# A one-core transformer kernel on Trainium2: position bias in one matmul pass of 64 columns, its scratch reordered, latent transposes one step earlier, mask additions behind them

## The chip, the core and the metric

The kernel runs on one core of one Trainium2 chip. The metric is device time in microseconds (us), the median of several runs. The engines of the core are TensorE (PE, with its weight loads as PEld), VectorE (DVE), ScalarE (ACT), GpSimd (POOL) and SyncE (SP); each works through its own instructions in order and waits on semaphores for the others.

## The reference, cut to what matters

The program is two transformer blocks on 256 rows of width 2048: projections, attention heads of several kinds, a feed-forward part, and a final output. Everything is float32. The part that the change touches is in the second block, the sparse attention "a" (`dsa_attention`), whose logits get a bias that depends on the distance between query and key through 32 buckets and a table of 32 buckets by 8 heads:

```
bias = rel_table[t5_bucket(pq[:, :, None] - pk)]
logits = jnp.where(valid, logits + bias, -jnp.inf)
```

and `valid` keeps the 64 keys with the highest index score (and only earlier keys). Beside it runs the latent attention "b", whose query and key/value latents are normed and multiplied:

```
qb = rms_norm(bcq, g) @ w_b_uq
kv = rms_norm(bckv, g) @ w_b_ukv
```

## The kernel before

**Products.** Each weight matrix is streamed in groups of 2 x 128 rows by 512 columns (512 KB). SP loads a group into one of four RAW slots. ACT copies it rounded into WH (`split`, L958), DVE subtracts to get the rest WL (`split`, L1409), and PE makes three 512-column matmuls per tile of it, high by high, high by low and low by high (L604 to L606), 12 in a group. That is how a float32 product is reached from the reduced format fp32r. ACT and DVE split group p + 4 in the step in which PE works on group p, so that PE has up to four groups in hand. `prod_free` and the pairs of PSUM banks 0 to 3 carry finished products to their evacuation (L963, L972). Every other piece of work (heads, norms, transposes, bias) is hung between groups: a table or an `if p == ...` in each engine's part says behind which group `p` it stands. No scheduler decides anything: the order is the order of the code.

**Position bias.** In the stage `gates_ret` (two passes of a loop, 16 groups each) twelve bias steps run behind groups 2, 4, 7, 10, 12 and 15 (`BIAS_AT`). For each, POOL writes the distances DI of 8 queries by 128 keys for four partition groups (L509), DVE turns them into one-hot rows OH with two instructions (L1586, L1587) two groups earlier, PE multiplies OH by the table REL (L748), ACT copies the result from PSUM to BE (L1132) and issues its store to `bias_scratch` in DRAM (L1134). REL holds the table rounded (part 0) and its remainder (part 1), 32 columns each. For each half of OH both parts are multiplied into the same 32 PSUM partitions: four matmuls a step. Before its copy ACT waits for the landing of the previous store (`bias_stored`).

**Reading it back.** When the heads "c" are finished, at the start of stage `b_proj` (24 groups), ACT issues four loads of the whole bias into BIAS, 128 queries by 8 heads by 384 (L1279).

**Stage `gates_b0`** (8 groups, p = 0 to 7) follows `b_proj`. DVE ends the search for the 64 best keys in steps 0 and 1, makes the mask in step 2 (L1804, L1805) and adds it to both halves of BIAS in steps 3 and 4 (L1813), after `bias_loaded`. The six tiles of the latents are transposed by PE behind groups 4, 5 and 6 (L645), copied by ACT (L999) and finished by DVE (L1438) into LATT in the same steps. Behind the stage PE waits until all six are done (`tr_lo`), before `merge_c`. ACT applies Silu to the b gate, 2048 elements a partition, in step 2 (L1330), and in step 7 evacuates the product with Sigmoid (L972).

**Stage `merge_c`** is a loop of two passes of 24 groups, four "a" heads each. For the first head POOL needs both mask additions (`sel_ready` 2) and writes QK (L560, L562); PE transposes QK behind group 0 (L665), ACT copies it to QKT (L1010), PE computes the scores behind group 1 (L685), DVE adds BIAS and finds the maximum (L1454 to L1461), ACT takes Exp (L1018). The four head steps of PE hang at groups 0, 1, 3, 4.

ACT can evaluate only functions of the table set that is loaded: where the next one is of another set, the compiler places an ACT_TABLE_LOAD. Silu, Sigmoid and Exp are in different sets here.

## Time and profile before

| what | us |
|---|---|
| median of 3 runs | 2494.52 (2493.90 to 2494.82) |
| profiled execution | 2494.93 |
| its span, first to last instruction | 2493.1 |
| PE busy | 2472.4 (99%) |
| DVE busy | 1502.3 (60%) |
| ACT busy | 1232.2 (49%) |
| POOL busy | 235.9 (9%) |

The share of busy time is that of the whole span. A matmul's busy time contains its latency: a 512-column matmul shows 0.39 us, but the next one begins 0.23 us after it, so that the distance between starts, not the duration, is what one costs. The rows of the trace come in the section before the prediction. A row of the timeline gives start, duration, engine, line, operation, what is written and read, shapes and how many; in brackets stands the idle time before it on its engine and what ended it.

### The profile page before, as it was taken

The page shows a single profiled execution, that of the slowest core. Times are in us where ns is not written, and L with a number is a line of the kernel's source. Part 1 is how long each engine was busy: PE and PEld are TensorE (multiplying, and loading weights), DVE is VectorE, ACT ScalarE, POOL GpSimd, SP SyncE. Part 2 cuts the span into 40 slices and gives each one's busy share as a digit, 9 for nine tenths or more (in the row PEclk, how much of TensorE's full clock was granted, in tenths as well). Part 3 has the DMA queues.
Part 4 walks back from the last instruction along what each step waited for, and adds up shares of the span by engine and source line. Part 5 has one row for each costly group of instructions (what it writes and reads, how often), then busy time and mean ns, then how long its engine had stood idle before and what let it go on. Part 6 is the DMA issues. An engine that isn't in the chain of part 4 may idle for free.

```text
span 2493.1 us, 35940 instructions
## 1 busy us (share of the span) xinstructions
PE 2472.4 (99%) x11882; PEld 2052.0 (82%) x11882; DVE 1502.3 (60%) x1800; ACT 1232.2 (49%) x1632; POOL 235.9 (9%) x277
## 2 busy tenths in 40 slices
PE   7999999999999999999999999999999999999999
PEld 6888888878888888888888888888887788877887
DVE  4444545486656777777777776444457655554564
ACT  4444555545445444444444445454547555555443
POOL 0012124231000000000000000010101000432000
PEclk9999999999999999999999999999999999999999
DMA  6555555566655555555555556554564545544655
GB/s 230 194 185 171 174 171 175 170 217 204 211 186 177 186 188 189 186 186 191 187 186 191 186 187 210 204 185 169 175 206 163 175 161 180 165 155 148 226 183 164
DMA packets 130194, 461.08 MB, mean 185 GB/s; under 512 B 14288, under 2 KB 17616, under 8 KB 129232
## 3 DMA queue, kind: packets, MB, share of 16 engines
q1 hardware_dynamic: 121536, 443.60, 53.1%
q10 hardware_dynamic: 8592, 16.58, 2.0%
q8 instruction: 44, 0.72, 0.1%
q14 instruction: 22, 0.18, 0.0%
HBM read 454.36 MB, written 5.77 MB: 185 GB/s over the span
## 4 chain that ended last, share of the span: by engine, by line
PE 97%; DVE 1%; ACT 1%; DMA 0%; issue 0%; ACTq 0%; POOL 0%; SPq 0%; POOLq 0%; DVEq 0%
PE PS L604 21%; PE PS L606 21%; PE PS L605 21%; PE PS L809 13%; PE PS L811 7%; PE PS L833 3%; PE PS L835 3%; PE PS L834 3%; PE PS L685 1%; PE PS L702 1%; PE PS L665 1%; PE PS L645 1%; DVE WL L1409 0%; PE PS L748 0%; PE PS L693 0%; ACT WH L958 0%
## 5 line engine op out<-in xcount | busy, mean ns | idle before, releaser
L1409 DVE TENSOR_TENSOR WL<-RAW,WH 128x1024 fp32r<-128x1024 f32 x842 | 1055.9, 1257 | 933.9 <-ACT WH L958 929.4
L958 ACT ACTIVATE WH<-RAW 128x1024 fp32r<-128x1024 f32 x842 | 890.2, 1059 | 1146.6 <-PE PS L606 755.0
L604 PE MATMUL PS<-WH,HT 128*128 128x512 f32 (+1 forms) x1820 | 726.8, 399 | 3.2 <-DVE LATT L1438 1.3
L606 PE MATMUL PS<-WH,HT 128*128 128x512 f32 (+1 forms) x1820 | 710.0, 390 | 0.0
L605 PE MATMUL PS<-WL,HT 128*128 128x512 f32 (+1 forms) x1820 | 708.6, 389 | 0.0
L809 PE MATMUL PS<-HT,WH 128*128 128x512 f32 x1408 | 498.2, 399 | 0.0
L604 PEld LDWEIGHTS PS<-WH,HT 128*128 128x128 f32 x1820 | 342.4, 188 | 77.1 <-issue 8.9
L606 PEld LDWEIGHTS PS<-WH,HT 128*128 128x128 f32 x1820 | 342.1, 188 | 72.4
L605 PEld LDWEIGHTS PS<-WL,HT 128*128 128x128 f32 x1820 | 342.9, 188 | 66.0
L811 PE MATMUL PS<-HT,WL 128*128 128x256 f32 x1408 | 395.4, 281 | 0.0
L809 PEld LDWEIGHTS PS<-HT,WH 128*128 128x128 f32 x1408 | 264.6, 188 | 65.7
L811 PEld LDWEIGHTS PS<-HT,WL 128*128 128x128 f32 x1408 | 266.0, 189 | 0.3
L833 PE MATMUL PS<-WH,ACTT 128*128 128x512 f32 x352 | 137.2, 390 | 0.0
L835 PE MATMUL PS<-WH,ACTT 128*128 128x512 f32 x352 | 137.1, 389 | 0.0
L834 PE MATMUL PS<-WL,ACTT 128*128 128x512 f32 x352 | 137.0, 389 | 0.0
L604 PE MATMUL PS<-WH,U 128*128 128x512 f32 x320 | 129.7, 405 | 0.0
L606 PE MATMUL PS<-WH,U 128*128 128x512 f32 x320 | 125.2, 391 | 0.0
L605 PE MATMUL PS<-WL,U 128*128 128x512 f32 x320 | 124.7, 390 | 0.0
L440 POOL TENSOR_TENSOR MS<-MS,CONST 128x2 f32<-128x2 f32 (+1 forms) x8 | 1.6, 200 | 1068.7 <-ACT PS L990 784.6
L835 PEld LDWEIGHTS PS<-WH,ACTT 128*128 128x128 f32 x352 | 66.1, 188 | 14.1
L833 PEld LDWEIGHTS PS<-WH,ACTT 128*128 128x128 f32 x352 | 66.1, 188 | 13.9
L834 PEld LDWEIGHTS PS<-WL,ACTT 128*128 128x128 f32 x352 | 66.1, 188 | 13.4
(242 smaller groups left out, 1922.2 us busy)
## 6 DMA issues: line engine op xcount, KB each, us to landing
RAW<-w_stream SPq DMA_DIRECT2D x842, 512.0 KB, 3.3
X<-x_in SPq DMA_DIRECT2D x2, 1024.0 KB, 6.6
MEMR<-mem_in ACTq DMA_DIRECT2D x1, 2048.0 KB, 11.3
X<-x_in ACTq DMA_DIRECT2D x4, 512.0 KB, 4.3
x_scratch<-X ACTq DMA_DIRECT2D x4, 512.0 KB, 4.1
X<-x_scratch ACTq DMA_DIRECT2D x1, 2048.0 KB, 8.1
out<-X ACTq DMA_DIRECT2D x8, 256.0 KB, 3.1
bias_scratch<-BE ACTq DMA_DIRECT2D x12, 128.0 KB, 2.4
```

What stands on the lines that cost most here:

```text
L604: pe.matmul(o, hi, WH[:, slot, kk, 0:cols], start=k == 0, stop=False)
L605: pe.matmul(o, hi, WL[:, slot, kk, 0:cols], start=False, stop=False)
L606: ins = pe.matmul(o, lo, WH[:, slot, kk, 0:cols], start=False, stop=k == nq * GK - 1)
L645: ins = pe.transpose(PS[:, 4 + at % 4, t * P:(t + 1) * P], src[:, t, k * P:(k + 1) * P], ident)
L665: ins = pe.transpose(PS[0:n, 4 + a, c * S + t * P:c * S + (t + 1) * P], QK[:, a, t, c * P:c * P + n], ident)
L809: pe.matmul(PS[:, half + f, :], WH[:, slot, kk, f * P:(f + 1) * P], HT[:, k, :, :], start=k == 0, stop=False, skip_group_check=True)
L811: ins = pe.matmul(PS[:, half + f, 0:S], WL[:, slot, kk, f * P:(f + 1) * P], HT[:, k, 0, :], start=False, stop=k == KT - 1, skip_group_chec ...
L833: pe.matmul(o, hi, WH[:, slot, kk, :], start=k == 0, stop=False)
L834: pe.matmul(o, hi, WL[:, slot, kk, :], start=False, stop=False)
L835: ins = pe.matmul(o, lo, WH[:, slot, kk, :], start=False, stop=k == FT - 1)
L958: act.activation(WH[:, g.slot(j)], RAW[:, g.slot(j)], ACT.Copy).then_inc(hi_split, 1)
L1409: dve.tensor_tensor(WL[:, s], RAW[:, s], WH[:, s].bitcast(F32), ALU.subtract).then_inc(lo_split, 1)
```

## The change

It does five things.

1. A bias step multiplies OH once by both parts of REL as 64 columns, two matmuls instead of four. The two partial results lie in 64 PSUM partitions and are not added there. ACT copies 64 partitions of the same length, and the store is 256 KB instead of 128 KB.
2. `bias_scratch` is ordered by query, row, segment, key. The store writes pieces of 128 elements (512 B). The load reads 3072 elements in one row (12 KB) per partition, for part 0 into BIAS and for part 1 into the new tile BIASL: eight loads of 384 KB instead of four. BIASL lies where JUNK lay, so the squares of the latents write to LSQ.
3. DVE adds BIASL to BIAS in two instructions, in steps 10 and 12 of `b_proj`.
4. The latent transposes stand behind groups 3, 4 and 5 of `gates_b0` (on PE, ACT and DVE). The mask additions stand in steps 5 and 6, the first behind the last LATT.
5. ACT's Silu of the b gate stands in step 7 of `gates_b0`, behind the Sigmoid evacuation, instead of in step 2.

```diff
@@ -223,6 +223,8 @@
         BIAS = sb("BIAS", [P, REL_HEADS, CAUS], F32, at_u2)
+        BIASL = sb("BIASL", [P, REL_HEADS, CAUS], F32, at_u1)
+        LSQ = sb("LSQ", [P, 832], F32, at_u1 + 12 * KB)
         LATT = sb("LATT", [P, 6, 2, S], F32R, at_sgx + 4 * KB)
 
         SG = {"merge_moba": sb("SG_MOBA", [P, T, CH], F32, at_u2), "merge_c": sb("SG_C", [P, T, CH], F32, at_u2 + 12 * KB),
@@ -243,7 +245,7 @@
 
         DI = sb("DI", [P, 8, P], I32, at_x)
         OH = sb("OH", [P, 2, 8, P], F32R, at_x + 4 * KB)
-        BE = sb("BE", [32, 8, P], F32, at_x + 12 * KB)
+        BE = sb("BE", [64, 8, P], F32, at_x + 12 * KB)
@@ -263,7 +265,7 @@
-        bias_scratch = nc.dram_tensor("bias_scratch", (32, 3, 32, P), F32, kind="Internal").ap()
+        bias_scratch = nc.dram_tensor("bias_scratch", (32, 64, 3, P), F32, kind="Internal").ap()
         x_scratch = nc.dram_tensor("x_scratch", (S, D), F32, kind="Internal").ap()
 
         def con(name, rows=P):
@@ -744,9 +746,8 @@
                 pe.wait_ge(onehot, k.count(1))
                 pe.wait_ge(bias_copied, k.count(1))
                 for b in range(2):
-                    for part in range(2):
-                        ins = pe.matmul(PS[0:32, 4 + b, :], REL[:, part, :],
-                                        OH[:, k.base % 2, 4 * b:4 * b + 4, :].rearrange("p q s -> p (q s)"), start=part == 0, stop=part == 1)
+                    ins = pe.matmul(PS[0:64, 4 + b, :], REL[:].rearrange("p a n -> p (a n)"),
+                                    OH[:, k.base % 2, 4 * b:4 * b + 4, :].rearrange("p q s -> p (q s)"), start=True, stop=True)
                 ins.then_inc(bias_done, 1)
             pe.wait_ge(rel_lo, 1)
             product_loop("gates_ret", 2, [(GD, HT)] * 2, bias_step)
@@ -894,9 +895,9 @@
             products("b_proj", [(GD, HT)] * 3, 0, index_step)
 
             def latent_tiles(_, p):
-                if 4 <= p < 7:
+                if 3 <= p < 6:
                     pe.wait_ge(lat_rows, 1)
-                    transposes("lat", PB, [2 * p - 8, 2 * p - 7])
+                    transposes("lat", PB, [2 * p - 6, 2 * p - 5])
 
             def a_step(i, p):
                 r = p // 6
@@ -1129,9 +1130,10 @@
                 k = At(s, i, len(BIAS_AT))
                 act.wait_ge(bias_done, k.count(3))
                 act.wait_ge(bias_stored, k.count(1) * 16)
-                act.activation(BE[:].rearrange("p (b q) s -> p b (q s)", b=2), PS[0:32, 4:6, :], ACT.Copy).then_inc(bias_copied, 1)
+                act.activation(BE[:].rearrange("p (b q) s -> p b (q s)", b=2), PS[0:64, 4:6, :], ACT.Copy).then_inc(bias_copied, 1)
                 act.wait_ge(bias_copied, k.count(2))
-                act.dma_start(bias_scratch[:, s % 3, ds(i * 16 + s // 3 * 8, 8), :], BE[:]).then_inc(bias_stored, 16)
+                act.dma_start(bias_scratch[ds(i * 16 + s // 3 * 8, 8), :, s % 3, :].rearrange("q r k -> r q k"),
+                              BE[:]).then_inc(bias_stored, 16)
 
             act.wait_ge(head_out, RET0 + 4 + 1)
             act.dma_start(MEMR[:], rows(mem_in)).then_inc(mem_loaded, 16)
@@ -1275,9 +1277,11 @@
 
             act.wait_ge(head_out, C0 + 4 + 1)
             act.wait_ge(bias_stored, 16 * (NBIAS + 1))
-            for g in range(4):
-                act.dma_start(BIAS[32 * g:32 * g + 32, :, :].rearrange("p h (s k) -> p h s k", s=3),
-                              bias_scratch[8 * g:8 * g + 8].rearrange("h s p k -> p h s k")).then_inc(bias_loaded, 16)
+            for part, dst in enumerate((BIAS, BIASL)):
+                for g in range(4):
+                    r = 32 * part + 8 * g
+                    act.dma_start(dst[32 * g:32 * g + 32].rearrange("p h n -> p (h n)"),
+                                  bias_scratch[:, r:r + 8].rearrange("p h s k -> p (h s k)")).then_inc(bias_loaded, 16)
 
             squares = [(PAC[:, h // 4, t, h % 4 * P:(h % 4 + 1) * P], MST[:, 0, t, h:h + 1]) for h in range(8) for t in range(T)]
             squares += [(PAC[:, 2, t, h * P:(h + 1) * P], MST[:, 1, t, h:h + 1]) for h in range(2) for t in range(T)]
@@ -1300,9 +1304,9 @@
                     for src, acc in squares[4 * (p - TOPK_AT - 1):4 * (p - TOPK_AT)]:
                         link(act.activation(JK[:, 0:P], src, ACT.Square, scale=P ** -0.5, accum_out=acc))
             def latent_squares(t):
-                act.activation(JUNK[:, t, 0:512], PB[:, t, 0:512], ACT.Square, scale=512 ** -0.5, accum_out=MS[:, t:t + 1])
-                act.activation(JUNK[:, t, 512:768], PAC[:, 7, t, KV_LAT], ACT.Square, scale=1 / 16.0, accum_out=MS[:, 2 + t:3 + t])
-                return act.activation(JUNK[:, t, 768:832], PAC[:, 7, t, KPE], ACT.Square, scale=192 ** -0.5,
+                act.activation(LSQ[:, 0:512], PB[:, t, 0:512], ACT.Square, scale=512 ** -0.5, accum_out=MS[:, t:t + 1])
+                act.activation(LSQ[:, 512:768], PAC[:, 7, t, KV_LAT], ACT.Square, scale=1 / 16.0, accum_out=MS[:, 2 + t:3 + t])
+                return act.activation(LSQ[:, 768:832], PAC[:, 7, t, KPE], ACT.Square, scale=192 ** -0.5,
                                       accum_out=MS[:, 4 + t:5 + t])
             act.wait_ge(prod_free, 2 + PROD0["b_proj"])
             for p in range(3 * GD):
@@ -1326,10 +1330,10 @@
                         steps(p)
 
             def latent_steps(p):
-                if p == 2:
+                if p == 7:
                     act.activation(PB[:, :, PB_Z:PB_Z + W], PB[:, :, PB_Z:PB_Z + W], ACT.Silu).then_inc(gate_ready, 1)
-                elif 4 <= p < 7:
-                    transposed("lat", LATT, [2 * p - 8, 2 * p - 7], "lat")
+                elif 3 <= p < 6:
+                    transposed("lat", LATT, [2 * p - 6, 2 * p - 5], "lat")
             gates_b("gates_b0", 0, 1, latent_steps)
 
             def a_step(i, p):
@@ -1787,6 +1791,10 @@
                                                            op0=ALU.mult, op1=ALU.add)
                         link(ins)
                     dve.sem_inc(idx_sum, 1)
+                if p in (10, 12):
+                    dve.wait_ge(bias_loaded, 128)
+                    half = slice((p - 10) * 2, (p - 10) * 2 + 4)
+                    link(dve.tensor_tensor(BIAS[:, half], BIAS[:, half], BIASL[:, half], ALU.add))
                 if p == TOPK_AT - 2:
                     dve.wait_ge(lat_rstd, 1)
                     for t in range(T):
@@ -1805,11 +1813,10 @@
                     link(dve.scalar_tensor_tensor(out=SC[:, 0:CAUS], in0=left[:, 0:CAUS], scalar=-NEG, in1=con("mask"),
                                                   op0=ALU.mult, op1=ALU.add))
 
-                if 4 <= p < 7:
-                    transposed("lat", LATT, [2 * p - 8, 2 * p - 7], "lat")
-                if p in (3, 4):
-                    dve.wait_ge(bias_loaded, 64)
-                    half = BIAS[:, (p - 3) * 4:(p - 2) * 4]
+                if 3 <= p < 6:
+                    transposed("lat", LATT, [2 * p - 6, 2 * p - 5], "lat")
+                if p in (5, 6):
+                    half = BIAS[:, (p - 5) * 4:(p - 4) * 4]
                     dve.tensor_tensor(half, half, SC[:, 0:CAUS].unsqueeze(1).broadcast_to([P, REL_HEADS // 2, CAUS]),
                                       ALU.add).then_inc(sel_ready, 1)
             dve.wait_ge(sel_ready, 2)
```

What stands in a row on the engines, before and after. On PE, one bias step between two groups (`gates_ret`). Before:

```order
L744 ISA
L748 MATMUL PS<-OH,REL 32x512 x4
L591 REGISTER_ALU
L604 MATMUL PS<-WH,HT 128x512
L605 MATMUL PS<-WL,HT 128x512
L606 MATMUL PS<-WH,HT 128x512
```

After:

```order
L746 ISA
L749 MATMUL PS<-OH,REL 64x512 x2
L593 REGISTER_ALU
L606 MATMUL PS<-WH,HT 128x512
L607 MATMUL PS<-WL,HT 128x512
L608 MATMUL PS<-WH,HT 128x512
```

Four matmuls have become two, and nothing else moved there. On DVE, `gates_b0` from the mask on (LATT is the latents' tile, SC the mask). Before:

```order
L1804 TENSOR_SCALAR OF<-OF 128x384
L1805 SCALAR_TENSOR_TENSOR SC<-OF,CONST 128x384
L1409 TENSOR_TENSOR WL<-RAW,WH 128x1024
L1813 TENSOR_TENSOR BIAS<-BIAS,SC 128x1536
L1409 TENSOR_TENSOR WL<-RAW,WH 128x1024
L1438 SCALAR_TENSOR_TENSOR LATT<-PS,PARAM,LATT 128x256 x2
L1813 TENSOR_TENSOR BIAS<-BIAS,SC 128x1536
L1409 TENSOR_TENSOR WL<-RAW,WH 128x1024
L1438 SCALAR_TENSOR_TENSOR LATT<-PS,PARAM,LATT 128x256 x2
L1409 TENSOR_TENSOR WL<-RAW,WH 128x1024
L1438 SCALAR_TENSOR_TENSOR LATT<-PS,PARAM,LATT 128x256 x2
L1409 TENSOR_TENSOR WL<-RAW,WH 128x1024
```

After:

```order
L1812 TENSOR_SCALAR OF<-OF 128x384
L1813 SCALAR_TENSOR_TENSOR SC<-OF,CONST 128x384
L1413 TENSOR_TENSOR WL<-RAW,WH 128x1024
L1442 SCALAR_TENSOR_TENSOR LATT<-PS,PARAM,LATT 128x256 x2
L1413 TENSOR_TENSOR WL<-RAW,WH 128x1024
L1442 SCALAR_TENSOR_TENSOR LATT<-PS,PARAM,LATT 128x256 x2
L1413 TENSOR_TENSOR WL<-RAW,WH 128x1024
L1442 SCALAR_TENSOR_TENSOR LATT<-PS,PARAM,LATT 128x256 x2
L1820 TENSOR_TENSOR BIAS<-BIAS,SC 128x1536
L1413 TENSOR_TENSOR WL<-RAW,WH 128x1024
L1820 TENSOR_TENSOR BIAS<-BIAS,SC 128x1536
L1413 TENSOR_TENSOR WL<-RAW,WH 128x1024
```

Each LATT pair stands one split earlier, and both mask additions stand behind the last pair, with one split left. On ACT, the end of `gates_b0` and the head of the `merge_c` loop (SGX is the Sigmoid evacuation, PB the b gate under Silu, QKT the first head's operand). Before:

```order
L972 ACT_TABLE_LOAD
L972 ACTIVATE SGX<-PS 128x1024
L1096 UNCONDITIONAL_BRANCH
L1096 ISA
L957 ISA
L958 ACTIVATE WH<-RAW 128x1024
L1004 ISA
L1010 ACTIVATE QKT<-PS,PARAM 128x256 x2
L957 REGISTER_ALU
L958 ACTIVATE WH<-RAW 128x1024
L1015 REGISTER_ALU
L1018 ACT_TABLE_LOAD
```

After:

```order
L973 ACT_TABLE_LOAD
L973 ACTIVATE SGX<-PS 128x1024
L1334 ACT_TABLE_LOAD
L1334 ACTIVATE PB<-PB 128x2x1024
L1097 UNCONDITIONAL_BRANCH
L1097 ISA
L958 ISA
L959 ACT_TABLE_LOAD
L959 ACTIVATE WH<-RAW 128x1024
L1005 ISA
L1011 ACTIVATE QKT<-PS,PARAM 128x256 x2
L958 REGISTER_ALU
```

Between the Sigmoid and the first split of the loop there now stand Silu and two table loads. The load that stood ahead of Exp in the loop's first head has moved to the loop's head, ahead of the first split, in both passes.

## Rows read from the trace of the kernel before

**Rows 1.** The chain that ended last, by engine, from the page.
```profile
PE 97%; DVE 1%; ACT 1%; DMA 0%; issue 0%; ACTq 0%; POOL 0%; SPq 0%; POOLq 0%; DVEq 0%
```

**Rows 2.** Timeline, PE and PEld: first bias step; weight loads of first and second.
```profile
504.69 1.09 PE L748 MATMUL PS<-OH,REL 128*32 128x512 f32 x4
505.62 0.40 PE L604 MATMUL PS<-WH,HT 128*128 128x512 f32 x1
...
504.51 0.75 PEld L748 LDWEIGHTS PS<-OH,REL 128*32 128x32 f32 x4
...
510.85 0.80 PEld L748 LDWEIGHTS PS<-OH,REL 128*32 128x32 f32 x4
```

**Rows 3.** Timeline, DVE and POOL between the first and the second one-hot.
```profile
503.18 1.29 DVE L1587 SCALAR_TENSOR_TENSOR OH<-DI,CONST,OH 128x1024 fp32r<-128x1024 int32 x1
504.68 4.06 DVE L1409 TENSOR_TENSOR WL<-RAW,WH 128x1024 fp32r<-128x1024 f32 x2 [0.22 <-DVE OH L1587]
...
504.78 2.88 POOL L509 TENSOR_TENSOR DI<-POSB 128x1024 int32<-128x1024 int32 x1 [5.65 <-DVEq L1590]
...
509.44 1.28 DVE L1587 SCALAR_TENSOR_TENSOR OH<-DI,CONST,OH 128x1024 fp32r<-128x1024 int32 x1
```

**Rows 4.** Timeline, the third bias step: its one-hot and its first weight load.
```profile
517.96 1.29 DVE L1587 SCALAR_TENSOR_TENSOR OH<-DI,CONST,OH 128x1024 fp32r<-128x1024 int32 x1
...
519.96 0.80 PEld L748 LDWEIGHTS PS<-OH,REL 128*32 128x32 f32 x4
```

**Rows 5.** Timeline, second pass of the loop: ACT's first split, seventh one-hot and step.
```profile
549.22 1.06 ACT L958 ACTIVATE WH<-RAW 128x1024 fp32r<-128x1024 f32 x1 [1.36 <-PE PS L606]
...
552.24 1.29 DVE L1587 SCALAR_TENSOR_TENSOR OH<-DI,CONST,OH 128x1024 fp32r<-128x1024 int32 x1
...
553.67 0.80 PEld L748 LDWEIGHTS PS<-OH,REL 128*32 128x32 f32 x4
```

**Rows 6.** Landing of the bias stores (page, median us) and of BIAS's four loads.
```profile
bias_scratch<-BE ACTq DMA_DIRECT2D x12, 128.0 KB, 2.4
...
DMA to landing us min/median/max: 4.9/9.3/16.8
```

**Rows 7.** Timeline, DVE's split of step 11 of `b_proj`.
```profile
1884.69 1.22 DVE L1409 TENSOR_TENSOR WL<-RAW,WH 128x1024 fp32r<-128x1024 f32 x1 [2.59 <-ACT WH L958]
```

**Rows 8.** Timeline, `gates_b0` into `merge_c`: PE, DVE's second mask addition, POOL's QK.
```profile
1944.65 0.49 PE L604 MATMUL PS<-WH,HT 128*128 128x512 f32 x1 [1.26 <-DVE LATT L1438]
...
1950.70 0.81 PE L685 MATMUL PS<-QKT 128*128 128x128 f32 x4
...
1938.51 1.75 DVE L1813 TENSOR_TENSOR BIAS<-BIAS,SC 128x1536 f32<-128x1536 f32 x1
...
1941.83 0.62 POOL L562 TENSOR_TENSOR QK<-PAC,MST 128x256 f32 x1
```

**Rows 9.** Timeline, ACT there; then ACT at the loop head of `a_proj`.
```profile
1943.49 1.06 ACT L958 ACTIVATE WH<-RAW 128x1024 fp32r<-128x1024 f32 x1 [1.42 <-PE PS L606]
...
1945.86 1.03 ACT L972 ACTIVATE SGX<-PS 128x1024 f32<-128x1024 f32 x1
...
1948.67 0.82 ACT L1010 ACTIVATE QKT<-PS,PARAM 128x256 f32<-128x256 f32 x2
...
1654.95 1.92 ACT L1256 ACTIVATE PB<-PB 128x2048 f32<-128x2048 f32 x1
1656.88 1.28 ACT L958 ACT_TABLE_LOAD   x1
1658.18 1.06 ACT L958 ACTIVATE WH<-RAW 128x1024 fp32r<-128x1024 f32 x1
```

**Rows 10.** Timeline, ACT's first split in the second pass of `merge_c`.
```profile
2023.14 1.06 ACT L958 ACTIVATE WH<-RAW 128x1024 fp32r<-128x1024 f32 x1 [1.89 <-PE PS L606]
```

**Rows 11.** Timeline, PE's first group of the program and what follows it.
```profile
17.36 0.80 PE L604 MATMUL PS<-WH,HT 128*128 128x512 f32 x1 [1.22 <-DVE HT L1438]
...
22.65 0.84 PE L645 MATMUL PS<-CONST,ROWS 128*128 128x128 f32 x4
```

## The prediction

> **What bounds the kernel now.** I read the page first. The chain that ended last is PE in 97% of the span [rows 1], so the end moves only with what PE issues and with what PE waits for. Busy time overstates a matmul, so I take distances between starts from PE's timeline. In the rows of the first bias step, see that PE goes from the bias matmuls to the next product without a gap, and how close the one-hot of DVE ends before PE wants it [rows 2, 3]. Then I read the one place in the touched stages where PE is idle, the end of `gates_b0` [rows 8], and what ACT does there [rows 9].
>
> **Two matmuls less in each bias step.** Four bias matmuls take PE from 504.69 to 505.62, 0.93 us, so one costs 0.23 [rows 2]. The number of columns that stream is 512 before and after; the weights become 64 columns wide, and weight loads lie beside the matmul ahead of them. So a step saves 2 x 0.233 = 0.47 us, and twelve steps 5.6 us, if PE finds its operands in time.
>
> **It will not, in three steps.** The first one-hot ends at 503.18 + 1.29 = 504.47, and PE's weight load follows at 504.51, 0.04 later. It normally stands 0.23 ahead of its matmul, here 0.18, so this step is already at its limit [rows 2, 3]. The second one-hot ends at 509.44 + 1.28 = 510.72, 6.25 after the first, and PE loads at 510.85 [rows 2, 3]. What fills these 6.25 us? After the one-hot DVE does two splits, the second of which ends at 504.68 + 4.06 = 508.74. POOL's distances end at 504.78 + 2.88 = 507.66, and 1.08 later the split ends, which is about one split. So DVE's second split stood until POOL was done [rows 3]. Nothing in this chain waits for PE, and the change takes nothing out of it. PE will now need 6.39 - 0.47 = 5.92 us between these two steps. It would load at 510.38 but gets the one-hot at 510.72 + 0.04: late by 0.38, less 0.05 that the load may be short, 0.33.
>
> The Trainium skill (SBUF — State Buffer, on the shared port pair) says that a VectorE operation with two SBUF inputs and a GpSimd operation exclude each other for the whole instruction. The trace agrees (the split ends 1.08 after POOL). A proportional sharing would let DVE move ahead with PE, and the bias steps would then give the full 5.6.
>
> In the second pass ACT begins late: its split at 549.22 [rows 5] follows PE's group that ended two groups before the bias matmul at 553.67 + 0.23 = 553.90. A group is 2.73, half of 510.85 + 0.23 - 505.62 [rows 2], so it ended at 548.44. ACT was held there by the evacuation, the copy to BE, the store and the turn of the loop, which begin with the end of group 15, before the bias step. They do not get shorter while PE arrives 0.47 sooner. The seventh one-hot ends at 552.24 + 1.29 = 553.53, PE's load now stands at 553.67 and would stand at 553.20 [rows 5]: late by 0.33 again, after the same 0.05. The eighth step follows after two groups as the second does, and pays the same 0.33. Together 1.0 us.
>
> The other steps have room: the third one-hot ends at 519.25, the load is at 519.96, 0.71 later [rows 4]. There the one-hot follows splits that follow PE's own groups, with no bias step between, so the distance stays. Steps 5 and 11 come two groups after another and lose 6.25 - 5.92 = 0.33 of that 0.71. **Bias stage: 5.6 - 1.0 = 4.6 us less.**
>
> **Copy and store.** ACT's copy has the same length in each partition, 1.0 us (as the Sigmoid of that size, [rows 9]). The store becomes 512 pieces of 512 B. It landed in 2.4 us before; a load of 768 such pieces needed at least 4.9 [rows 6]. In proportion between them I take 4 us. ACT waits for it before the next copy, at the closest 5.92 less about 1.2 for copy and issue, 4.7 later. Nothing waits then. Beyond that, ACT's splits queue behind it. The issue itself may last 0.2 longer, which would count in the seventh step alone.
>
> **Loads and additions.** Eight loads of 12 KB rows take the place of four of 512 B pieces: twice the bytes, a twelfth of the pieces. The last of the four landed after 16.8 us [rows 6], beside the weight stream and with no wait of PE. The new ones are needed at step 10 of `b_proj`, ten groups of 2.73 us after the issue. DVE's additions have the size of a mask addition, 1.75 us [rows 8], and each stands in a gap of 2.59 [rows 7]. Nothing is queued in it, so they cost nothing; without the gap they would take their 1.75 from four groups in hand. I take zero, between -0.5 (less time in the issue on ACT) and +2.
>
> **The wait for LATT goes.** PE stood 1.26 us behind `gates_b0` until the last LATT [rows 8]. With the transposes one step earlier and DVE's mask additions behind, the last LATT is done near 1940.6 (estimate: ACT's copy behind PE's group 5 at 1937.3, a split, a pair), and PE goes on at 1943.3. That alone gives 1.3.
>
> **What is late next.** POOL makes the first head's QK after the second mask addition. Before, the addition ended at 1940.26 and QK at 1941.83 + 0.62 = 1942.45, 2.2 later [rows 8]. Now two additions and a split stand behind the last LATT, so the second ends near 1945.1 and QK near 1947.3, while PE wants it behind group 0 of `merge_c`, at 1946.0. So PE gives back the 1.3 there.
>
> Then comes ACT. Its last split in `gates_b0` stays at 1943.49, since PE's work up to there is the same. Sigmoid's table is loaded, Sigmoid ends at 1945.86 + 1.03 = 1946.89 [rows 9]. The order of the changed kernel then shows: table, Silu, table, split, QKT. At the head of `a_proj` ACT did Silu, table, split in one run: 1.93 from Silu to the table load, 1.30 from the load to the split [rows 9]. So: 1946.89 + 1.30 + 1.93 + 1.30 = 1951.42 for the split, 0.97 more to QKT (1.06 less the overlap), 0.82 for it, and PE can compute scores near 1953.3. Before it did at 1950.70, with QKT ready since 1949.49 [rows 8, 9]. **Cost 2.6 us**, and it swallows the waits for LATT and QK. Nothing later regains it: PE has no other wait in `merge_c`. The second pass loads its table in a gap of 1.89 ahead of the first split, so it costs nothing [rows 10], as the load needs only ACT itself.
>
> The Trainium skill (ScalarE: Activation LUTs, What ACT_TABLE_LOAD costs) prices a switch at 2.66, with a drain of 1.38 behind the load. The rows show the next operation 1.30 after it [rows 9]. By the page two more switches (and the one before Sigmoid unchanged) would make the cost 5.4.
>
> **Sum.** 2494.93 (profiled) - 4.6 + 2.6 = 2492.9. The median of the runs is 0.4 below the profiled one: 2492.5.
>
> **The rivals.** *The moved Silu is covered* (a load runs while ACT waits or the scores have more room than I see). Then only POOL's QK holds PE and the stage costs 0, so the time is 2494.5 - 4.6 = 2489.9, or 2488.9 if the bias steps pay no waits either. Against it: ACT's run is a plain sum of measured pieces, 3.8 us beyond its end of before, with 1.2 of room. For it: 1950.12 is reached with pieces from another stage.
>
> *PE's clock falls.* After the long wait at the start the first group took 22.65 - 17.36 = 5.29 us instead of 2.73, so its spacing fits 1.2 GHz instead of 2.4 [rows 11]. A wait of 1.26 left it at the higher level [rows 8]. The new wait before the scores, 2.6 with 1.3 shortly before, lies between. If it decides beyond 1.26, one group costs 2.6 more: 2495.1, slower than before.
>
> *The stores hold ACT.* If the pieces of 512 B land like the median load (9.3, [rows 6]), ACT stands 4.6 us at each of the four close steps, and with 0.7 of room PE loses up to 3.9 each: above 2500. It begins at a landing of 5.4. Against it: the share of a queue of four loads is in that median.
>
> *It does less than it says*: the 64-column matmul costs as much as two (0.23 more in each of 24). Then 2498. Weight loads of 128 columns cost nothing beside matmuls elsewhere, so hardly.
>
> *The page's price for a switch* gives 2495.3.
>
> **How the numbers follow.** Forecast 0.68, its own range 2491.3 to 2493.7 (bias waits 0.4 to 1.6, Silu's chain 2.2 to 3.0). Silu covered 0.13. Clock 0.08. Stores 0.03. Wide matmul 0.02. The page's price 0.02. The rest, 0.04, lies on both sides. The range for 8 in 10 goes to the covered Silu at 2489.9 and the clock at 2495.1: 2489.8 to 2495.3. A measurement of this kernel can tell about 0.2% (5 us) from no change. Faster by that, below 2489.5: half of the covered case and some rest, 0.10. Slower, above 2499.5: stores and rest, 0.05. Same: 0.85.
>
> **What would show it.** In the changed trace: bias steps 0.47 long, with three weight loads 0.04 behind a one-hot and PE idle about 0.3 at each; stores landing near 4 us; no wait for LATT; PE idle about 1.3 before the first transposes of `merge_c`, released by POOL, and about 2.6 before its first scores, released by ACT's QKT; three table loads between 1944 and 1952, each 1.3. It is wrong if ACT's split at the head of `merge_c` stands before 1949, or if a wait for ACT or DMA shows in `gates_ret`.

## The result and the profile after

| | before | after |
|---|---|---|
| median, us (9 runs each) | 2494.09 (2493.77 to 2495.23) | 2500.78 (2499.76 to 2503.19) |
| span of the profiled execution | 2493.1 | 2498.6 |

By medians that is 6.7 us slower (ratio 1.0026, 95% interval 1.0018 to 1.0034), where 2.0 us faster was forecast (2494.5 to 2492.5). The intervals here and below leave out two single executions far off the rest, one of 2717 us in the run a1 and one of 3072 us of the kernel before beside it. The spans of the two profiled executions differ by 5.5, and their traces say where that is. The chain that ended last, by engine, from the page of after (compare [rows 1]):

```profile
PE 97%; DMA 1%; DVE 1%; issue 1%; ACT 0%; ACTq 0%; POOL 0%; SPq 0%; DVEq 0%; POOLq 0%
```

DMA, 0% before, has 1% of the span. That is the first trace of the cause. I take four stretches, cut at PE's work that both kernels have.

**Bias stage, 4.1 us less.** The head transposes ahead of `b_proj` (L710 before, L712 after) begin at 1841.09 before and 1837.01 after. Of these 4.1 the bias stage itself makes 4.0: from PE's last work of other heads at 483.84 (L702) to the end of the twelfth step at 594.92 it is 111.08 us before, and from 483.71 (L704) to 590.83 it is 107.12 after. The start of the stage itself lies anywhere from 482.98 to 484.08 in the 16 profiles read, all alike up to there, so the last tenths of the 4.1 mean nothing. Timeline after, PEld, weight loads of the bias steps 1, 2, 7 and 8 (start, duration, in brackets the idle time; compare [rows 2, 5]):

```profile
504.39 0.31 PEld L749 LDWEIGHTS PS<-OH,REL 128*64 128x64 f32 x2
510.66 0.19 PEld L749 LDWEIGHTS PS<-OH,REL 128*64 128x64 f32 x2 [0.43 <-DVE OH L1591]
...
551.96 0.19 PEld L749 LDWEIGHTS PS<-OH,REL 128*64 128x64 f32 x2 [0.80 <-DVE OH L1591]
558.24 0.19 PEld L749 LDWEIGHTS PS<-OH,REL 128*64 128x64 f32 x2 [0.52 <-DVE OH L1591]
```

The step has shrunk by 0.47, and the second one waits for its one-hot; the load starts stand 6.27 us apart, which is the distance of the two one-hots (503.05 and 509.32 on DVE). Five steps wait, 2, 5, 7, 8 and 11, not three.

**`b_proj`, 5.3 us more.** This is what the prediction had at zero. Timeline after, ACT and its queue, then PE:

```profile
1842.10 2.33 ACTq L1283 DMA_DIRECT2D BIASL<-bias_scratch  x4
...
1857.55 1.06 ACT L959 ACTIVATE WH<-RAW 128x1024 fp32r<-128x1024 f32 x1 [7.20 <-DMA RAW<-w_stream]
...
1862.93 1.06 ACT L959 ACTIVATE WH<-RAW 128x1024 fp32r<-128x1024 f32 x1 [4.05 <-DMA RAW<-w_stream]
...
1858.93 0.50 PE L892 MATMUL PS<-QKT 64*128 64x128 f32 x4 [3.70 <-ACT QKT L1294]
...
1861.24 0.63 PE L608 MATMUL PS<-WH,HT 128*128 128x512 f32 x1
1861.67 0.63 PE L606 MATMUL PS<-WH,HT 128*128 128x512 f32 x1
```

ACT has no weights to split for 7.2 us. Its copy to QKT, an index head's operand, stands behind that split in its queue, so PE waits 3.7 us. Then the matmuls start 0.43 apart instead of 0.23, and from L892 to the seventh product matmul behind it PE needs 3.92 us (1858.93 to 1862.85), where one index step earlier, at the full clock, the same took 2.35 (1848.37 to 1850.72): 1.6 more. Together 5.3.

Why were the weights late? The DMA view of the 16 us from the first bias load on (queue: packets, MB, share of 16 engines; q1 carries the weights, q10 ACT's loads), after:

```profile
q10 hardware_dynamic: 311, 2.67, 74.2%
q1 hardware_dynamic: 304, 1.09, 26.4%
```

and before:

```profile
q10 hardware_dynamic: 3104, 1.56, 52.1%
q1 hardware_dynamic: 726, 2.61, 51.9%
```

The weights got 1.09 MB instead of 2.61. The weight loads of the window 1836 to 1885 us landed as follows, before and then after:

```profile
DMA to landing us min/median/max: 3.0/3.3/8.5
...
DMA to landing us min/median/max: 3.1/4.3/15.8
```

The bias loads after landed as follows (BIAS, then BIASL):

```profile
DMA to landing us min/median/max: 6.2/8.4/11.2
...
DMA to landing us min/median/max: 13.3/16.1/18.8
```

They were not late themselves (the first addition needs them at 1883.25); they made others late.

**`gates_b0` to the scores, 2.6 us more, as forecast.** Timeline after, ACT, then PE (compare [rows 8, 9]):

```profile
1945.81 1.28 ACT L973 ACT_TABLE_LOAD   x1
1947.11 1.02 ACT L973 ACTIVATE SGX<-PS 128x1024 f32<-128x1024 f32 x1
1948.15 1.28 ACT L1334 ACT_TABLE_LOAD   x1
1949.44 1.92 ACT L1334 ACTIVATE PB<-PB 128x2048 f32<-128x2048 f32 x1
1951.38 1.28 ACT L959 ACT_TABLE_LOAD   x1
1952.67 1.06 ACT L959 ACTIVATE WH<-RAW 128x1024 fp32r<-128x1024 f32 x1
1953.64 0.82 ACT L1011 ACTIVATE QKT<-PS,PARAM 128x256 f32<-128x256 f32 x2
...
1948.62 0.66 PE L667 MATMUL PS<-CONST,QK 128*128 128x128 f32 x4 [1.26 <-POOL QK L564]
...
1954.51 1.34 PE L687 MATMUL PS<-QKT 128*128 128x128 f32 x4 [2.47 <-ACT QKT L1011]
```

The wait for LATT is gone, POOL's takes its place, and then ACT's chain of table load, Silu, table load, split.

**Behind the scores, 1.6 us more.** Windows of 4 us after (length; then busy time of PE, PEld, DVE, ACT, POOL; granted clock; DMA share; GB/s), two of `b_proj` and two around the scores:

```profile
1856.00:1860.00 4.00, 1.07 (x8) 0.64 (x8) 1.36 (x2) 1.33 (x2) 0.00 (x0) 0.91 0.90 205
1860.00:1864.00 4.00, 4.00 (x14) 3.06 (x13) 1.27 (x4) 1.07 (x2) 0.00 (x0) 0.66 1.02 387
1952.00:1956.00 4.00, 1.53 (x6) 1.30 (x6) 1.79 (x2) 3.39 (x5) 0.00 (x0) 0.86 0.00 0
1956.00:1960.00 4.00, 4.00 (x14) 3.14 (x13) 1.74 (x4) 1.15 (x5) 0.00 (x0) 0.71 0.77 261
```

The granted clock falls behind both long waits; where the matmuls stand 0.43 apart instead of 0.23, it is at the level of 1.2 GHz. From the scores at 1954.51 to the seventh product matmul behind them is 3.70 us (to 1958.21). The same stretch takes 2.15 at the full clock (1954.83 to 1956.98 in a second profile of the same program, the run c3 below).

The sum: -4.1 + 5.3 + 2.6 + 1.6 = +5.4, against 5.5.

### The profile page after: what moved, and what is told of

Its sections match the earlier page's. It is cut to its first block, busy times and chain, and to the rows that moved or that the text cites. A ratio compares the mean times of both kernels' runs of the same rounds, so it can differ in the third digit from the quotient of the medians.

```text
span 2498.6 us, 35901 instructions
## 1 busy us (share of the span) xinstructions
PE 2471.1 (99%) x11858; PEld 2051.5 (82%) x11858; DVE 1508.9 (60%) x1802; ACT 1233.4 (49%) x1633; POOL 235.3 (9%) x277
## 4 chain that ended last, share of the span: by engine, by line
PE 97%; DMA 1%; DVE 1%; issue 1%; ACT 0%; ACTq 0%; POOL 0%; SPq 0%; DVEq 0%; POOLq 0%
PE PS L606 21%; PE PS L608 21%; PE PS L607 21%; PE PS L810 13%; PE PS L812 7%; PE PS L834 3%; PE PS L836 3%; PE PS L835 3%; PE PS L687 1%; PE PS L704 1%; PE PS L647 1%; PE PS L667 1%; DMA RAW<-w_stream 1%; PE PS L695 0%; PE PS L712 0%
## 5 line engine op out<-in xcount | busy, mean ns | idle before, releaser
L836 PEld LDWEIGHTS PS<-WH,ACTT 128*128 128x128 f32 x352 | 66.1, 188 | 14.1
```

Source lines behind the costliest of these rows:

```text
L836: ins = pe.matmul(o, lo, WH[:, slot, kk, :], start=False, stop=k == FT - 1)
```

## The experiments

Three things cost: the loads, ACT's chain, the clock. First theory: rows of 12 KB hold up the weight stream. Rival: it is the 3.15 MB, whatever their rows. The kernel before was timed beside each set, at 2494.2 to 2494.8; each ratio is against that.

### The two halves apart

`a1_bias_only` is the changed kernel with `gates_b0` (latents, Silu, mask additions) as before; `a2_latents_only` is the kernel before with those alone changed.

The diff is a1's, against the changed kernel.

```diff
-                if p == 7:
+                if p == 2:
                     act.activation(PB[:, :, PB_Z:PB_Z + W], ...)
-                elif 3 <= p < 6:
+                elif 4 <= p < 7:
```

> The changed kernel with stage gates_b0 as before (transposes behind groups 4 to 6, mask additions in steps 3 and 4, Silu in step 2); bias steps, scratch, loads and DVE additions as changed. Theory (two separate losses): the bias steps give 4.1 us, the loads cost 5.3 (a wait of 3.7 for a weight group that landed late and some 1.6 at the lower clock behind it), so about 2495.4, 5.4 below the changed kernel. Rival (the move in gates_b0 is the whole loss and the wait for the weights is chance of one execution): about 2490.

> The kernel before with only gates_b0 changed (transposes one step earlier, mask additions in steps 5 and 6, Silu in step 7). Theory: 2.6 us until the first scores of merge_c and 1.7 behind them at the lower clock, so about 2498.4. Rival (the waits there come from DVE being late after the loads): 2494 or below.

Measured: a1 2496.43 us, ratio 1.0009 (0.9999 to 1.0019), 1.0 over the theory and not clear of no change; PE waits 3.5 for QKT in L892, and the granted clock is 0.77 behind it. a2 2498.26, ratio 1.0016 (1.0006 to 1.0025); the waits of 1.3 and 2.5 ahead of the scores are there, with the lower clock behind. So the bias half loses its own gain in `b_proj`, and the half of the latents is a plain loss. By medians the two make 1.65 + 3.48 = 5.1 us; the whole showed 6.7 in nine runs and 4.8 in a later single one. In a2, with the loads of before, PE waits 0.4 in L891 too: there the issue of the last two loads lasted 4.93 us (2.66 before) and held ACT's splits.

### The loads: spread out, or in short rows

`a3_spaced_loads` issues one load behind each of the first eight groups of `b_proj`; `a4_short_rows` pads the scratch to four segments, so that all eight loads, still at once, read pieces of 1.5 KB.

```diff
# a3
+                if p < 8:
+                    bias_load(p)
# a4
-        bias_scratch = nc.dram_tensor("bias_scratch", (32, 64, 3, P), ...)
+        bias_scratch = nc.dram_tensor("bias_scratch", (32, 64, 4, P), ...)
-                              bias_scratch[:, r:r + 8].rearrange("p h s k -> p (h s k)")
+                              bias_scratch[:, r:r + 8, 0:3, :].rearrange("p h s k -> p h (s k)")
```

> The changed kernel with its eight bias loads issued one behind each of the groups 0 to 7 of b_proj instead of all at its start; same bytes, same rows of 12 KB. Theory (the loads in a row keep the weight stream off the DMA engines): no wait for weights, 5.3 us less, about 2495.5, weight loads landing within 6 us. Rival (a single 12 KB row ahead of the weights is enough): still 2 us or more of waits in b_proj.

> The changed kernel with the scratch padded from 3 to 4 segments, so that the same eight loads at the same place read pieces of 1.5 KB instead of rows of 12 KB; same bytes landed. Theory (row length decides who gets a DMA engine next): weights land in time and the wait in b_proj goes, about 2495.5. Rival (the 3.1 MB are what costs, in whatever pieces): about 2500.8 with the wait for weights as now.

Measured: a3 2494.07 us, ratio 0.9998 (0.9988 to 1.0007), with no wait of ACT for weights and none of PE in `b_proj`. a4 2494.21, ratio 0.9999 (0.9989 to 1.0009); ACT waits three times for weights, 3.4 us at most, and PE 0.8. Either median is 6.6 to 6.7 us below that of the changed kernel, more than the 5.3 of `b_proj`, and 1.3 to 1.4 below the theory. For a3 the clock behind the scores fits, which stayed at 1.00 in its profile; in a4's it fell (0.72), and the profiled execution took 2495.40. The loads were the cause, and their time was not fixed by their bytes alone.

### The kernel before with double bytes, and with long rows

`b2_double_pieces` issues the four loads of before twice, the second time into BIASL: 3.15 MB in pieces of 512 B. `b3_long_rows_half` reads 1.57 MB in rows of 12 KB.

```diff
# b2
+            for part, dst in enumerate((BIAS, BIASL)):
                 for g in range(4):
# b3
+                act.dma_start(BIAS[32 * g:32 * g + 32].rearrange("p h n -> p (h n)"), flat[g])
```

> The kernel before with its four loads of the bias issued twice, into two tiles, in the same pieces of 512 bytes: the 3.15 MB that the changed kernel reads, but not its rows of 12 KB; nothing else is changed, and the second tile is read by nobody. Theory (the rows of 12 KB hold up the weight stream): with short pieces the weight loads keep landing in about 4.2 us, ScalarE waits for w_stream no more than before, and the time is that of before, 2494.5, range 2493.5 to 2496; the second four loads land late, over 25 us. Rival (it is the 3.15 MB, whatever their rows): ScalarE waits for w_stream for over 3 us in b_proj, matmuls of L892 wait for QKT, and the time is 2497 to 2500.

> The kernel before with its four loads reading whole rows of 12 KB, one per partition, 1.57 MB in all as before; since the scratch is not in that order, the bias values stand at other positions than in the reference, and nothing else differs. Theory (long rows hold up the weight stream while they last): half as many rows of 12 KB as in the changed kernel, so ScalarE waits for w_stream once or twice, some 3 to 7 us in b_proj instead of 13, and as the first wait of such a length was covered for some 3.5 us by buffers, the time is 0 to 3 us over before, 2494.5 to 2497.5, best value 2496. Rival (it is the number of bytes): 1.57 MB cost nothing as before, no wait for w_stream over 2 us, time within 0.5 us of before.

Measured: b3 2494.51 us, ratio 1.0001 (0.9991 to 1.0010); one wait of ACT for weights of 2.4, which PE did not feel: the time of the rival (bytes), with a wait as the theory (rows) had it. b2 2504.98, ratio 1.0045 (1.0029 to 1.0060), more than either theory allowed. Its timeline, ACT and its queue, then PE:

```profile
1847.58 10.00 ACTq L1282 DMA_DIRECT2D BIASL<-bias_scratch  x4
1857.70 2.00 ACT L960 ACTIVATE WH<-RAW 128x1024 fp32r<-128x1024 f32 x2 [12.05 <-issue]
...
1860.30 0.80 PE L893 MATMUL PS<-QKT 64*128 64x128 f32 x4 [8.00 <-ACT QKT L1293]
```

Here nobody waited for weights (they landed within 8.6 us). ACT was held for 12 us in the issue itself: the last four loads, of 768 pieces each, took 10.0 us to issue, where the four long ones of the changed kernel took 2.33. So b2 doesn't compare bytes; it shows another cost, a rival that I had not set up. b3 says that long rows alone, at half the bytes, cost nothing. Double the bytes in short pieces, without that hold of ACT, stay untested.

### ACT's chain ahead of the scores

`b1_silu_early` is a3 with the Silu back in step 2; `c1_silu_first` leaves it in step 7, but ahead of the Sigmoid evacuation.

```diff
# b1
-                if p == 7:
+                if p == 2:
# c1: in step 7, this line now stands behind the Silu
                     evacuations(name, At(GROUP0[name]), 0, p, count, lambda c: gate_chunk(chunk * CH + c), ACT.Sigmoid)
```

> The run with the spaced loads (2494.07 against a before of 2494.78 on the same chip), with one edit: the forward Silu stands in step 2 of gates_b0 again, as in the kernel before; the latents stay one step forward and the mask additions behind them. Theory: the Silu in step 7, with the table loads around it, is what pushes the QK^T copy that releases the scores 2.5 us late. Back in step 2 it lies in time that ScalarE has to spare, so the wait for QKT in front of the scores (2.5) goes, the 1.3 us wait of LATT stays away, POOL's 1.3 stays: 0.7 + 2.6 = 3.3 us under before, 2491.2, range 2490.5 to 2492.5. Rival: the QK^T chain is late because the latents and Sigmoid of the same steps crowd ScalarE, whatever the Silu does: the wait for QKT stays over 1.5 us and the time stays within 1 us of 2494.

> The spaced loads again (2494.07), with one edit: the forward Silu stays in step 7 of gates_b0, but ahead of the evacuations that use the Sigmoid instead of behind them. Both use another activation table than the steps around them; what changes is only the order in which ScalarE takes them up and so the number of table loads on its chain. Theory: of the 2.5 us that the scores wait for QKT, the two table loads around the Silu (about 1.3 each) are the larger part; with the Silu first they lie in earlier idle time, the wait falls to 0 to 1 us and the time to 2491.5 (range 2490.5 to 2493). Rival: the Silu's own 1.9 us on the chain is what counts, since it stays ahead of the same QK^T copy: the wait stays over 2 us and the time within 0.8 us of 2494.

Measured: b1 2490.33 us, ratio 0.9984 (0.9975 to 0.9993); c1 2490.58 (2489.91 to 2495.34), ratio 0.9988 (0.9979 to 0.9998). In both, PE waits 1.3 for POOL and not at all for QKT. Their scores stand 3.5 earlier than a3's (1945.99 and 1946.03 for 1949.54), of which 0.9 was there at 483 us already; the other 2.6 is the wait. Timeline of c1, ACT, then PE:

```profile
1938.89 1.06 ACT L959 ACTIVATE WH<-RAW 128x1024 fp32r<-128x1024 f32 x1 [1.66 <-PE PS L608]
1939.86 1.90 ACT L1336 ACTIVATE PB<-PB 128x2048 f32<-128x2048 f32 x1
1941.78 1.28 ACT L973 ACT_TABLE_LOAD   x1
1943.07 1.02 ACT L973 ACTIVATE SGX<-PS 128x1024 f32<-128x1024 f32 x1
1943.99 1.05 ACT L959 ACTIVATE WH<-RAW 128x1024 fp32r<-128x1024 f32 x1
1944.94 0.83 ACT L1011 ACTIVATE QKT<-PS,PARAM 128x256 f32<-128x256 f32 x2
...
1946.03 0.82 PE L687 MATMUL PS<-QKT 128*128 128x128 f32 x4
```

The Silu is on the same chain with its 1.9 us. What went from this chain are two table loads of 1.28: there is none between the split at 1938.89 and the Silu (the last load before it is at 1903.15), nor ahead of the split at 1943.99. The load for Exp stands behind the next split again, at 1947.30, where ACT then still waits 1.1 us for DVE. The order of the two functions was the fault, not the step.

### Everything mended

`b4_best` is b1 with the mask additions in steps 3 and 5, and the bias steps behind groups 3, 5, 8, 10, 13 and 15, with their one-hots made three groups ahead.

```diff
-        BIAS_AT = (2, 4, 7, 10, 12, 15)
+        BIAS_AT = (3, 5, 8, 10, 13, 15)
-                k = At(BIAS_AT.index(p + 2), i, len(BIAS_AT))
+                k = At(BIAS_AT.index(p + 3), i, len(BIAS_AT))
-                if p in (5, 6):
+                if p in (3, 5):
```

> The changed kernel with three things put right at once: the loads spread one behind each of the first eight groups of b_proj; the forward Silu in step 2 of gates_b0 again, with the mask additions in steps 3 and 5 behind the latents; the six position bias steps at 3, 5, 8, 10, 13, 15 with their one-hots made three groups ahead, so that TensorE needn't wait for them. Theory: the bias steps give their whole 12 x 0.47 = 5.6 us (only 4.1 came through, 1.5 was waits for one-hots), LATT gives 1.3: 2494.6 - 6.9 = 2487.7, range 2486.5 to 2490. Rival: one-hots made earlier hold VectorE before copies that others wait for (the shifted order of VectorE costs 1 to 2 us), so that the bias stage gives 3 to 4 us as it does in the changed kernel: 2489.5 to 2491.5.

Measured: 2487.34 us, ratio 0.9972 (0.9961 to 0.9983): 6.9 less than before beside it, as the sum said. No weight load of a bias step waits (compare the four rows of after):

```profile
506.32 0.36 PEld L749 LDWEIGHTS PS<-OH,REL 128*64 128x64 f32 x2
512.22 0.36 PEld L749 LDWEIGHTS PS<-OH,REL 128*64 128x64 f32 x2
```

They stand 5.90 apart, which is the 5.92 that the prediction had worked out for steps without a wait. The one-hots of these two steps are still 6.27 apart (502.32 and 508.59), but early enough. From the same two points as above the stage takes 105.32 us (482.98 to 588.30), 5.8 less than before. POOL's QK is done at 1937.93 + 0.61 = 1938.54, before PE's transposes at 1939.35, and that wait of 1.3 has gone too.

### Repeats: is it settled?

Then the spaced loads were profiled once more on another chip, together with the changed kernel.

> The spaced loads once more, unchanged, for one profile: behind the same two waits of TensorE (1.3 and 2.5 us) in front of the scores the granted clock stayed at 1.0 in its first profile, while it fell to 0.72 and 0.85 in two neighbouring windows of 4 us in the profiles of the short rows and of the latents alone, and to 0.86 and 0.71 in the changed kernel. If the fall is a matter of chance from execution to execution, this profile may show it (half and half), about 1.5 us then; if it follows from the program, the clock is 1.0 again. Time 2494, within 2 us.

> The changed kernel once more, unchanged, for one profile. If the lower clock behind the scores is a matter of chance, it may be missing here, and the matmuls there stand 0.22 us apart instead of 0.43, with a span shorter by 1.5 us; if it follows from the program, the two windows of 4 us show about 0.86 and 0.71 again. The lower clock behind the wait of 3.7 us in b_proj is expected in either case. Time 2500.8, within 2 us.

Measured: the spaced loads took 2499.87 us, nearly all of the loss again and 6 over what was expected. The waits of that profile in `b_proj` (us in total, times, longest):

```profile
ACT WH L959 <- DMA RAW<-w_stream: 9.4, 4, 3.4
...
PE PS L892 <- ACT QKT L1294: 2.8, 1, 2.8
```

The changed kernel took 2499.45, with 3.2 in L892 and the lower clock behind it (0.50 in the window 1860 to 1864), but the full clock behind its scores. So I timed the kernels again, on a fourth chip, with one new: `d1_short_spaced`, b4 with pieces of 1.5 KB (the edit of a4).

> The best kernel so far (2487.34) with one edit: its spread loads read pieces of 1.5 KB (four rows of 512 bytes kept for each head and query, three read) instead of whole rows of 12 KB, for the same 3.15 MB. Theory (a queue with longer rows takes more of the DMA engines from the weight stream): the weight loads land at least as early as with long rows, at most about 7 us, on any chip, no wait for w_stream, 2487.3, range 2486.3 to 2488.5. Rival (only the 3.15 MB in some 27 us count, whatever the rows): no difference from the long rows beside it on the same chip, in time and in landings of the weights, and where those wait, so does this.

> The spaced loads a third time, unchanged, timed. Once all ten runs lay between 2493.6 and 2494.8; on another chip one profiled run took 2499.87, with four waits for w_stream (3.4 us the longest), a wait of 2.8 us in L892 and a lower clock behind the scores. If spaced long rows stand at the edge of what the DMA engines can give beside the weights, the runs fall in two groups here or lie between 2494 and 2500, by the chip; if the one long run was chance, the median is 2494.1 within 0.8 again. A clock of 1.0 behind the scores is expected where the whole is near 2494, and 0.7 to 0.9 where it is over 2495.5.

> The best kernel unchanged, on another chip: in its one profile the weight loads landed within 7.1 us, ahead of the 10 us that cost nothing. Theory: it needs no luck, since b_proj stands earlier by 3 us only and the loads land as they did: 2487.3 within 1 us. Rival: it is at the same edge as the spaced loads, and the runs reach 2491 to 2493 where waits for w_stream come back.

> The changed kernel with pieces of 1.5 KB, all eight loads at once, unchanged, on another chip: 2494.21 with runs from 2493.0 to 2496.5 before. Theory (short pieces leave the weight stream its larger share): again 2494.2 within 1.5 us, weight loads landing within 13 us, the wait of L892 under 1.5 us. Rival (the first result was the luck of that chip, and it is the 3.15 MB that cost): 2498 to 2501 here, with a wait of over 3 us in L892 as in the changed kernel.

Measured:

| kernel | us, median (lowest to highest), runs | ratio (interval) |
|---|---|---|
| d1, short rows, spaced | 2486.85 (2486.64 to 2488.31), 6 | 0.9970 (0.9957 to 0.9982) |
| d2, a3 again | 2493.71 (2493.35 to 2498.39), 10 | 1.0000 (0.9991 to 1.0010) |
| d3, b4 again | 2487.86 (2486.64 to 2494.16), 10 | 0.9977 (0.9967 to 0.9986) |
| d4, a4 again | 2495.12 (2494.03 to 2498.05), 10 | 1.0003 (0.9994 to 1.0013) |

With spaced long rows, d2 has two of its ten runs at 2498 and d3 one, 7 us over its lowest; c1, also with them, had two of ten at 2495, 4 over its median. They stand at an edge. Short rows at once took 0.1 (a4 against a3) and 1.4 us (d4 against d2) more than spaced long ones, each pair beside each other on one chip. All 20 runs of a4 and d4 lie below 2498.1, all ten of the changed kernel above 2499.4. d1 has the lowest median and no long run in six, but b4 had none in seven either: that is too few to show that d1 has left the edge. Its latest landing of weights is 8.2 us against 8.7 in d3, so its rival, that short rows change nothing once the loads are spaced, stands.

What the DMA engines moved in the 16 us from the first bias load on, and what followed in `b_proj`:

| profile | rows, issue | bias MB | weights MB | latest weights, us | PE wait for QKT |
|---|---|---|---|---|---|
| before | 0.5 KB, at once | 1.56 | 2.61 | 8.5 | none |
| b3 | 12 KB, at once | 1.57 | 2.63 | 10.5 | none |
| a2 | 0.5 KB, at once | 1.57 | 2.56 | 9.8 | 0.4, behind an issue of 4.9 |
| after | 12 KB, at once | 2.67 | 1.09 | 15.8 | 3.7 |
| a1 | 12 KB, at once | 2.41 | 1.21 | 16.9 | 3.5 |
| c3, after again | 12 KB, at once | 2.73 | 1.07 | 15.1 | 3.2 |
| a4 | 1.5 KB, at once | 2.43 | 1.46 | 12.5 | 0.8 |
| d4, a4 again | 1.5 KB, at once | 2.32 | 1.65 | 12.0 | none |
| a3 | 12 KB, spaced | 1.57 | 2.52 | 10.3 | none |
| d2, a3 again | 12 KB, spaced | 1.57 | 2.36 | 10.6 | none |
| c2, a3 again | 12 KB, spaced | 1.68 | 2.58 | 14.1 | 2.8 |
| d1 | 1.5 KB, spaced | 1.74 | 2.62 | 8.2 | none |
| d3, b4 again | 12 KB, spaced | 1.81 | 2.62 | 8.7 | none |

Both theories hold a part. The bytes: all kernels of the table move 3.6 to 4.4 MB in these 16 us, so whatever the bias takes is not there for the weights, which want 3.0 MB (188 GB/s, the mean of the window 1400 to 1800 us). This is what the mix moves and not a ceiling: after the bias loads are done, the window 1860 to 1864 above moves 387 GB/s at a like DMA share, nearly all of it weights. Why the mix moves less is open. The rows: at once and with the same 3.15 MB to load, long rows leave the weights 1.07 to 1.21 MB, rows of 1.5 KB 1.46 and 1.65. That reading has a rival that no run separates: the last four loads in short rows also took longer to issue (3.93 us in a4 and 3.29 in d4, against 2.04 to 2.33), so they came a little spread. Leaving a2 aside, PE does not wait up to a latest landing of 12.0 us; at 12.5 it begins; from 14 on it stands for about 3 us.

## Why the prediction was wrong, and where right

**The step that failed** is "Loads and additions. ... I take zero, between -0.5 ... and +2." It measured 5.3 us. The argument had two premises: the new loads are needed late, and the last of the old ones landed after 16.8 us beside the weight stream with no wait of PE. Both were true. It asked when the loads land, not what lands behind them. The row used as comfort, 1.57 MB beside the weights without a wait, was the case with half the bytes, and the DMA engines had no room for the other half at once: the weights' own landings at their latest, 8.5 us before, were not read. a1 shows the loss with the bias half alone, a3 and a4 take it away. Against the forecast the two spans differ by 5.5 + 2.0 = 7.5 us: 5.3 here, 1.6 for the clock behind the scores, which the sum left out, and 0.5 in the bias stage.

**The lower clock** was a rival with 0.08, at 2.6 us and behind the scores alone. It came true there and behind the wait in `b_proj`, at 1.6 each in the profile. Behind the scores it is not certain for a program: eight profiles have the same waits of 1.3 and 2.5 there, and five fell (after, a2, a4, c2, d4), three didn't (c3, a3, d2). The changed kernel and the spaced loads each show both. What decides between them is open.

**Bias stage**: 4.6 forecast, 4.0 to 4.1 measured. The 0.47 a step and the place of the waits at steps 2, 7 and 8 were right (the spacing of one-hots 6.27, forecast 6.25). The waits cost PE 12 x 0.47 - 3.96 = 1.7 us instead of 1.0: about 0.2 each at steps 2, 5 and 11, 0.4 at step 8 and 0.6 at step 7, where 0.33 each at three was forecast. Mis-sized was the issue of a store: "may last 0.2 longer". It takes 0.63 us for 0.32 before, in each step:

```profile
L1135 ACTq DMA_DIRECT2D bias_scratch<-BE x12: 625/632/737, 506.9 to 593.6; - x12
DMA to landing us min/median/max: 3.6/4.1/5.1
```

ACT's next split stands behind it (idle time 1.01 instead of 0.80 behind the third step), then DVE's, and so the fourth one-hot came 0.59 earlier than before (526.48 for 527.07) where the third came 0.82 earlier. That took the room that I had given to the steps 5 and 11; and at step 7, where the prediction let the issue count, its 0.31 more fit the 0.6. The chain is read, not tested. b4 shows that without the waits the loads stand 5.90 apart. The landing of 4 us was right (4.1; 2.4 before, [rows 6]), and no copy waited for a store. One sign that the prediction had named for being wrong did show in `gates_ret`: ACT waits 1.9 us for weights there once, behind the first store, where before it never did. PE did not wait for it. The Trainium skill's rule on the shared port pair (SBUF — State Buffer, Who interferes with whom) agrees with the spacing, which is 6.27 in the changed kernel and in b4, though PE arrives earlier.

**The additions** were free, as forecast: 1.75 us each, no one waits.

**LATT, POOL, Silu**: right by place and size. POOL's wait 1.26, forecast 1.3; the split of ACT at 1952.67 where 1951.42 was forecast, the chain having begun 1.24 later (1944.73 for 1943.49); the scores late by 2.57, forecast 2.6. b1 and c1 confirm it: without the two table loads the wait is not there, with the Silu on the chain (c1) or off it (b1). The price of 2.66 for a switch, from the Trainium skill (ScalarE: Activation LUTs, What ACT_TABLE_LOAD costs), didn't come: 1.29 to 1.30 from load to next operation, three times.

The rivals "stores hold ACT", "the matmul costs double" and "Silu covered" did not happen. Against the second speaks the step itself: 5.90 between loads in b4.

## What to carry to other kernels

Cost an added or moved transfer by what it takes from the streams beside it: its bytes and those of the stream against what the DMA engines moved with both at work (here 3.6 to 4.4 MB in 16 us), then the stream's latest landing against the slots in hand, before asking when the transfer itself is needed. Spread such a load over the groups, or cut it into shorter rows: either took most of the loss away here, though not in every execution. But count the pieces, since their issue holds the engine that issues them. Before a function of another table is moved, write down the order of functions around its new place: one place ahead or behind decides two table loads, and behind a late wait they reach the bottleneck.

## What was unexpected of the hardware

- Two queues with work did not share the DMA engines evenly by bytes. With eight loads of 12 KB rows issued, the weights (4 KB pieces, 512 KB a load) got 1.09 of 3.76 MB in 16 us; against rows of 1.5 KB 1.46 of 3.89 and 1.65 of 3.97.
- Issuing had a limit of its own: four loads of 384 KB in pieces of 512 B behind four others took 10.0 us of ACT's queue, the same bytes in rows of 12 KB 2.33. Twelve stores of 512 pieces took 0.63 us each to issue, against 0.32 for stores of 256.
- The granted clock fell, at a cost of 1.6 us, behind waits of 1.3 and 2.5 us in some executions of a program and not in others.
- The same program with spaced loads took 2493.4 to 2494.8 in 18 of 21 executions and 2497.9 to 2499.9 in three. In the one of the three that was profiled, weight loads took up to 14.1 us to land while the DMA engines moved no less in the first 16 us (2.58 MB of weights against 2.52 and 2.36). What slowed them afterwards is open.
